# Order of TensorE's work in the attention loop: the former item's products with the values ahead of the turning of the present item's probabilities

## The chip, the cores and the metric
The kernel runs on one core of one Trainium2 chip. Its time is that of one execution on the device in microseconds (us); a lower time is better. Three runs of the kernel before took 3362.86, 3367.79 and 3368.50 us, the median is 3367.79.

## What is computed
The reference runs two blocks over 256 tokens of width 1024, two layers each: modulated norms, mixers, dense feed-forwards and a mixture of experts. What matters here is attention, which stands in it in five forms: neighbourhood attention of 256 latent tokens over 256 latent and 256 context tokens, dense attention of the 256 context tokens, window attention with a sink, difference attention, and dilated attention in three groups. Each is of this form, per head and query:

```python
s = jnp.einsum('bhqd,bhkd->bhqk', q, k) * d ** -0.5 + bias
m = s.max(-1, keepdims=True)
e = jnp.exp(s - m)
p = e / e.sum(-1, keepdims=True)
o = jnp.einsum('bhqk,bhkd->bhqd', p.astype(v.dtype), v)
```

## The kernel before, in words
The program is written out by hand for each engine, and the engines meet at semaphores. SyncE loads weights in units of up to 1 MB into four buffers (`raw`), ScalarE rounds them to a high part, VectorE forms the low part, and TensorE multiplies activations with both. This weight stream fills most of the time (L302, L307, L356 to L360). It stands still in the attention loops, with its buffers full.

Attention is done in items. An item is one head, 128 queries (so two items per head) and all keys that these see. `attn_pe`, `attn_dve` and `attn_act` (from L948, L995 and L1023) are the same loop seen from TensorE, VectorE and ScalarE. They run five times, on lists made by `even_items` (E0: 16 items of 512 keys with a bias; E1: 16 of 256), `window_items` (W: 16 of 512 with a mask), `diff_items` (D: 16 of 512) and `dilated_items` (A: 24 of 128, then 24 of 256, two extra matmuls each). An item i passes through these steps:

- S(i), TensorE, `scores` (L963, L965): queries by keys into one of two PSUM banks `SC`, then the bias or mask is added by more matmuls.
- maximum, VectorE (L1015; in W L1012 and L1013, with the sink's floor).
- exponential, ScalarE (L1030), from PSUM into one of two tiles `prob`, with its sum read out after it.
- T(i), TensorE (L989): `prob` is turned in pieces of 128 x 128 into one of two PSUM banks `PT`.
- copy, VectorE (`take`, L1006): `PT` into one of two tiles `probT` in SBUF.
- O(i), TensorE, `outputs` (L976): `probT` is the operand that is loaded as weights, the values stream past it, and the result is added up in PSUM.

The tiles `prob` and `probT` lie in `tmp`, so the trace calls them tmp. A float32 matmul stands as two records in the trace, so O of four pieces stands as x8, and O of two pieces as x4.

The order on TensorE is that of the loop in `attn_pe`: S(0), then for each i S(i+1), T(i), O(i-1), and O of the last item at the end. VectorE's order is maximum of i, copy of i-1, maximum of i+1. In between it has other work at some items, given by `every`: in E0, E1 and D, after items 4 and 6, it splits a finished pair of operands for the next projection (L932, L933), and in A it carries a finished group of eight heads out of PSUM after items 9, 17, 25, 33 and 41 (L2000). After a loop VectorE normalises the results (from L1222, L1435 or L2011 on), having waited for the last O, and TensorE turns them (`heads_out_pe`, L1235) for the next projection.

TensorE's waits in the loop: S(i) waits until the exponential of i-2 has read its bank; T(i) for the exponential of i and, from i = 2, for the copy of i-2, which has read its bank; O(i) for the copy of i.

Of the kernel before, what the change touches and what calls it, by code (L numbers as in the profile page):

```python
# [134 lines left out]
def program(nc, a, out, plan):  # L135
# [6 lines left out]
    def sem(name):  # L142
        if name not in sems:
            sems[name] = ctx.enter_context(nc.semaphore(name))
        return sems[name]
# [802 lines left out]
    def attn_pe(e, base, items, ready, *deps):  # L948

        e.after(*deps)  # L950
        last = len(items)

        def scores(i):
            it = items[i]
            if ready:
                ready(e, i)
            if i >= 2:

                e.eng.wait_ge(sem("exp_done"), base + i - 1)
            bank = SC[i % 2]  # L960
            n = it["n"]
            adds = it["adds"]
            nc_last = nc.tensor.matmul(bank[:, 0:n], it["q"], it["k"], start=True, stop=not adds)  # L963
            for j, (l_, r_) in enumerate(adds):
                nc_last = nc.tensor.matmul(bank[:, 0:r_.shape[-1]], l_, r_, start=False, stop=j == len(adds) - 1)  # L965
            nc_last.then_inc(sem("scores"), 1)

        def outputs(i):
            it = items[i]

            e.eng.wait_ge(sem("probT_done"), base + i + 1)
            if it.get("o_free"):
                it["o_free"](e)
            kt = it["n"] // P
            for k in range(kt):
                ins = nc.tensor.matmul(it["o"], probT[i % 2][:, k * P:k * P + P], it["v"][k],  # L976
                                       start=k == 0, stop=k == kt - 1)
            ins.then_inc(sem("out_ready"), 1)

        scores(0)  # L980
        for i in range(last):
            if i + 1 < last:
                scores(i + 1)

            e.eng.wait_ge(sem("exp_done"), base + i + 1)
            if i >= 2:
                e.eng.wait_ge(sem("probT_done"), base + i - 1)
            for k in range(items[i]["n"] // P):
                ins = nc.tensor.transpose(PT[i % 2][:, k * P:k * P + P], prob[i % 2][:, k * P:k * P + P], ident)  # L989
            ins.then_inc(sem("prob_turned"), 1)  # L990
            if i >= 1:
                outputs(i - 1)
        outputs(last - 1)

    def attn_dve(e, base, items, floor, *deps, every=None):  # L995
# [1050 lines left out]
    with ctx:  # L2046
# [272 lines left out]
        def _(pe):  # L2319
# [13 lines left out]
            for st in range(2):  # L2333
                if st:
                    conv_pe(e, 1)

                def ready(e, i):
                    if st == 0 and i % NT == 0:
                        e.after(f"bias{i // NT}")
                attn_pe(e, ATT0[st], E_ITEMS[st], ready, "qkT1", f"convT{st}", "even zeros", f"odd zeros{st}")  # L2340
                heads_out_pe(e, f"att_e{st}")
                follow(e, s, f"cat_e{st}")
                project_pe(e, s, [(xhi, xlo, KD)], D, f"out_e{st}")
                resid_pe(e, f"res_e{st}", (pick_lat, pick_ctx)[st], 0)
# [6 lines left out]
            if on(3):  # L2351
                mod_pe(e, s, 1, f)
                for st, n in enumerate((OW, OW - OQ)):
                    norm_pe(e, f"in_o{st}")
                    follow(e, s, f"in_o{st}")
                    project_pe(e, s, [(xhi, xlo, KD)], n, f"in_o{st}", late_pe(e, s, 1, st))
                odd_qk_pe(e)
                attn_pe(e, ATT0[2], W_ITEMS, None, "ckT", "dkT")
                heads_out_pe(e, "att_w")
                attn_pe(e, ATT0[3], D_ITEMS, None, "att_w:oT")  # L2360
                heads_out_pe(e, "att_d")
                follow(e, s, "cat_o")
                project_pe(e, s, [(xhi, xlo, KD)], D, "out_o")
                resid_pe(e, "res_o", pick_lat, 0)
# [69 lines left out]
```

## Time and profile before

| | |
|---|---|
| median of three runs | 3367.79 us |
| profiled execution: its time, its span | 3368.8 us, 3366.9 us |
| busy: TensorE, VectorE, ScalarE | 89%, 57%, 47% of the span |
| TensorE's mean granted clock | 0.935 of full speed |
| loops, from the first S to the last O started, read in the order of time | E0 273 to 319, E1 367 to 394, W 1074 to 1129, D 1134 to 1180, A 3063 to 3124 us |

Rows of the order in time give the start of a group of records in us, its length, its engine (PE is TensorE's matmuls, PEld its weight loads, DVE VectorE, ACT ScalarE), line, operation, what is written from what, sizes, and how many records it joins; in brackets stands how long the engine had been idle before it, and what ended that. The length goes from the first start to the last end, and matmuls overlap: the next group starts before the former one ends.

### The profile page before, as it was taken

To read this page: it belongs to the slowest core of one execution; us is meant where nothing else is said; L and a number is where in the kernel's file an instruction comes from. 1 tells how busy PE (TensorE), PEld (TensorE's weight loads), DVE (VectorE), ACT (ScalarE), POOL (GpSimd) and SP (SyncE) were. 2 spreads that over 40 slices of the span, in tenths; PEclk is the share of its full clock that TensorE was granted. 3 is DMA by queue.
4 is the path that set the end of the run, shared out by engine and by line. 5 is a ranking of instruction groups with operands and counts; after the bars stand their busy time and mean duration, and the time that the engine had idled before them with its cause. 6 is when DMAs were issued, how large, how long until landed. Compare 5 with 4: busy or idle time off the path is not lost.

```text
span 3366.9 us, 37398 instructions
## 1 busy us (share of the span) xinstructions
PE 3007.6 (89%) x14027; PEld 2483.2 (74%) x14027; DVE 1912.1 (57%) x2235; ACT 1578.0 (47%) x2125; POOL 148.9 (4%) x195
## 2 busy tenths in 40 slices
PE   6997799899686979999999989989778989898698
PEld 5775578787474658888888878867667878787587
DVE  5565555556456456666666665546555555544555
ACT  4553344444453235555555544455434444445344
POOL 1002000000111000000000000000000000000000
PEclk8998899999787979999999999989889999999899
DMA  7571245456752025555556555534024544551243
GB/s 262 199 238 50 67 156 173 160 167 205 188 187 100 1 66 190 179 171 186 187 182 195 187 163 181 186 130 138 1 71 167 179 164 162 200 183 62 81 158 142
DMA packets 266638, 510.49 MB, mean 152 GB/s; under 512 B 9497, under 2 KB 40449, under 8 KB 266528
## 3 DMA queue, kind: packets, MB, share of 16 engines
q1 hardware_dynamic: 262576, 498.11, 44.5%
q0 software_dynamic: 3952, 10.89, 1.6%
q8 instruction: 72, 1.18, 0.1%
q14 instruction: 38, 0.31, 0.0%
HBM read 507.91 MB, written 1.05 MB: 151 GB/s over the span
## 4 chain that ended last, share of the span: by engine, by line
PE 83%; DVE 8%; ACT 4%; DMA 2%; POOL 1%; issue 1%; DVEq 0%; ACTq 0%; POOLq 0%
PE bank L356 24%; PE bank L357 23%; PE bank L360 23%; PE bank L963 2%; PE bank L976 2%; DVE wlo L307 2%; PE bank L1599 2%; PE bank L433 1%; PE bank L989 1%; DMA raw<-in_od_w_in 1%; ACT whi L302 1%; PE bank L738 1%; PE bank L965 1%; POOL ss L679 1%; PE bank L866 1%
## 5 line engine op out<-in xcount | busy, mean ns | idle before, releaser
L307 DVE TENSOR_TENSOR wlo<-raw,whi 128x1024 fp32r<-128x1024 f32 x1044 | 1267.9, 1224 | 984.1 <-ACT whi L302 978.9
L302 ACT ACTIVATE whi<-raw 128x1024 fp32r<-128x1024 f32 x1044 | 1098.6, 1060 | 1030.4 <-PE bank L360 975.6
L356 PE MATMUL bank<-whi,xhi 128*128 128x512 f32 (+2 forms) x2672 | 1024.1, 383 | 53.9 <-DVE wlo L307 34.4
L357 PE MATMUL bank<-wlo,xhi 128*128 128x512 f32 (+2 forms) x2672 | 1015.2, 380 | 0.0
L360 PE MATMUL bank<-whi,xlo 128*128 128x512 f32 (+2 forms) x2672 | 1014.0, 379 | 0.0
L356 PEld LDWEIGHTS bank<-whi,xhi 128*128 128x128 f32 x2672 | 511.7, 192 | 150.8 <-issue 52.7
L360 PEld LDWEIGHTS bank<-whi,xlo 128*128 128x128 f32 x2672 | 511.3, 191 | 89.0
L357 PEld LDWEIGHTS bank<-wlo,xhi 128*128 128x128 f32 x2672 | 512.2, 192 | 86.4
L356 PE MATMUL bank<-whi,f_hhi 128*128 128x512 f32 x880 | 350.0, 398 | 0.0
L360 PE MATMUL bank<-whi,f_hlo 128*128 128x512 f32 x880 | 348.8, 396 | 0.0
L357 PE MATMUL bank<-wlo,f_hhi 128*128 128x512 f32 x880 | 348.8, 396 | 0.0
L360 PEld LDWEIGHTS bank<-whi,f_hlo 128*128 128x128 f32 x880 | 165.7, 188 | 40.4
L357 PEld LDWEIGHTS bank<-wlo,f_hhi 128*128 128x128 f32 x880 | 165.8, 188 | 39.2
L356 PEld LDWEIGHTS bank<-whi,f_hhi 128*128 128x128 f32 x880 | 165.8, 188 | 39.1
L738 PE MATMUL bank<-kb,tmp 128*128 128x128 f32 x224 | 51.1, 421 | 100.1 <-DVE tmp L718 100.1
L517 DVE TENSOR_TENSOR f_hlo<-bank,f_hhi 128x512 fp32r<-128x512 f32 (+1 forms) x114 | 71.6, 668 | 120.1 <-ACT f_hhi L479 120.1
L1030 ACT ACTIVATE tmp<-bank,negm 128x512 f32<-128x512 f32 (+2 forms) x112 | 60.7, 542 | 149.2 <-DVE negm L1015 110.2
L738 PEld LDWEIGHTS bank<-kb,tmp 128*128 128x128 f32 x224 | 45.1, 224 | 107.9 <-DVE tmp L718 107.6
L479 ACT ACTIVATE f_hhi<-bank 128x512 fp32r<-128x512 f32 (+1 forms) x114 | 60.6, 581 | 127.4 <-PE bank L433 127.4
L356 PE MATMUL bank<-whi,spad 128*128 128x512 f32 x192 | 83.0, 432 | 24.7 <-DVE wlo L307 24.1
L489 ACT ACTIVATE tmp<-bank 128x512 f32<-128x512 f32 (+2 forms) x120 | 60.9, 561 | 66.9 <-PE bank L360 66.8
L1015 DVE TENSOR_REDUCE negm<-bank 128x1 f32<-128x256 f32 (+2 forms) x96 | 46.0, 480 | 74.1 <-PE bank L965 45.3
(377 smaller groups left out, 2229.9 us busy)
## 6 DMA issues: line engine op xcount, KB each, us to landing
raw<-in_ffn_w SPq DMA_DIRECT2D x180, 1024.0 KB, 5.0
raw<-in_moe_w SPq DMA_DIRECT2D x64, 1024.0 KB, 5.1
raw<-in_moe_w SPq DMA_DIRECT2D x80, 768.0 KB, 4.4
raw<-in_ada_w SPq DMA_DIRECT2D x48, 1024.0 KB, 5.2
raw<-in_ev_w_in SPq DMA_DIRECT2D x24, 1024.0 KB, 5.8
raw<-in_ffn_w SPq DMA_DIRECT2D x36, 512.0 KB, 3.6
raw<-in_hyb_w_in SPq DMA_DIRECT2D x18, 1024.0 KB, 4.8
raw<-in_attn_w_qkv SPq DMA_DIRECT2D x18, 1024.0 KB, 4.9
```

Source lines behind the costliest of these rows:

```text
L302: nc.scalar.activation(whi[s][:, :, :], raw[slot][:, 2 * j:2 * j + 2, :], ACT.Copy)\
L307: nc.vector.tensor_tensor(wlo[s][:, :, :], raw[slot][:, 2 * j:2 * j + 2, :], whi[s][:, :, :].bitcast(F32), ALU.subtract)\
L356: nc.tensor.matmul(bank[:, 0:n], xk_h, whi[s][:, wk, 0:n], start=first, stop=False)
L357: ins = nc.tensor.matmul(bank[:, 0:n], xk_h, wlo[s][:, wk, 0:n], start=False, stop=last and xl is None)
L360: ins = nc.tensor.matmul(bank[:, 0:n], xk_l, whi[s][:, wk, 0:n], start=False, stop=last)
L489: ins = nc.scalar.activation(sg[:, t, 0:n], G[t][:, 0:n], ACT.Silu)
L517: ins = nc.vector.tensor_tensor(hlo[:, at, :].rearrange(flat), T[b // TOK][:, 0:k * TOK], hhi[:, at, :].bitcast(F32).rearrange(flat), ALU. ...
L738: ins = nc.tensor.transpose(banks[b][:, c:c + P], tmp[:, t, kk * P:kk * P + P], ident)
L963: nc_last = nc.tensor.matmul(bank[:, 0:n], it["q"], it["k"], start=True, stop=not adds)
L976: ins = nc.tensor.matmul(it["o"], probT[i % 2][:, k * P:k * P + P], it["v"][k], start=k == 0, stop=k == kt - 1)
L1030: nc.scalar.activation(prob[i % 2][:, 0:it["n"]], SC[i % 2][:, 0:it["n"]], ACT.Exp, bias=negm[:, i:i + 1], accum_out=den[:, i:i + 1]).then ...
L1599: ins = nc.tensor.matmul(to, diagonal_tap(k, j), hpad[:, k, j:j + TOK], start=j == 0, stop=j == TAPS - 1)
```

## The change
In TensorE's loop O(i-1) moves ahead of T(i), so that the order is S(i+1), O(i-1), T(i). T's own wait for the copy of i-2 goes; O(i-2), which now always stands before T(i), has made that wait. The other engines' programs are as before.

```diff
@@ -981,15 +981,13 @@
         for i in range(last):
             if i + 1 < last:
                 scores(i + 1)
+            if i >= 1:
+                outputs(i - 1)
 
             e.eng.wait_ge(sem("exp_done"), base + i + 1)
-            if i >= 2:
-                e.eng.wait_ge(sem("probT_done"), base + i - 1)
             for k in range(items[i]["n"] // P):
                 ins = nc.tensor.transpose(PT[i % 2][:, k * P:k * P + P], prob[i % 2][:, k * P:k * P + P], ident)
             ins.then_inc(sem("prob_turned"), 1)
-            if i >= 1:
-                outputs(i - 1)
         outputs(last - 1)
```

## Rows read from the trace of the kernel before

**Rows 1.** The page's chain that ended last: shares of the span by engine.

```profile
PE 83%; DVE 8%; ACT 4%; DMA 2%; POOL 1%; issue 1%; DVEq 0%; ACTq 0%; POOLq 0%
```

**Rows 2.** Waits in E1, then A: engine, tile, line waited for: us, times, longest.

```profile
PEld bank L989 <- ACT tmp L1030: 8.1, 11, 3.5
...
PEld bank L989 <- ACT tmp L1030: 6.9, 16, 1.6
```

**Rows 3.** Order in time, E1, within the loop.

```profile
377.13 0.38 PE L989 MATMUL bank<-kb,tmp 128*128 128x128 f32 x2
...
377.67 0.41 DVE L1006 COPY tmp<-bank 128x256 f32<-128x256 f32 x1
...
379.40 0.41 DVE L1006 COPY tmp<-bank 128x256 f32<-128x256 f32 x1
...
388.23 0.61 PE L976 MATMUL bank<-e_p,tmp 128*128 128x128 f32 x4
...
388.67 0.60 PE L963 MATMUL bank<-e_kT,e_qT 128*128 128x256 f32 x2
...
389.11 0.38 PE L989 MATMUL bank<-kb,tmp 128*128 128x128 f32 x2
...
389.32 0.61 PE L976 MATMUL bank<-e_p,tmp 128*128 128x128 f32 x4
...
391.54 0.38 PE L989 MATMUL bank<-kb,tmp 128*128 128x128 f32 x2
```

**Rows 4.** Order in time, the end of E1.

```profile
392.82 0.44 PE L989 MATMUL bank<-kb,tmp 128*128 128x128 f32 x2 [0.45 <-ACT tmp L1030]
...
393.29 0.42 DVE L1006 COPY tmp<-bank 128x256 f32<-128x256 f32 x1 [0.80 <-PE bank L989]
...
393.77 0.52 PEld L976 LDWEIGHTS bank<-e_p,tmp 128*128 128x128 f32 x4 [0.26 <-DVE tmp L1006]
```

**Rows 5.** Order in time, A, items of 128 keys.

```profile
3070.44 0.33 PE L989 MATMUL bank<-kb,tmp 128*128 128x128 f32 x1
...
3077.84 0.29 DVE L1006 COPY tmp<-bank 128x128 f32<-128x128 f32 x1 [0.52 <-PE bank L989]
...
3090.00 0.27 PE L989 MATMUL bank<-kb,tmp 128*128 128x128 f32 x1
```

**Rows 6.** Order in time, A, items of 256 keys.

```profile
3092.45 0.38 PE L989 MATMUL bank<-kb,tmp 128*128 128x128 f32 x2
...
3102.69 0.41 DVE L1006 COPY tmp<-bank 128x256 f32<-128x256 f32 x1
...
3104.28 0.41 DVE L1006 COPY tmp<-bank 128x256 f32<-128x256 f32 x1
...
3121.36 0.38 PE L989 MATMUL bank<-kb,tmp 128*128 128x128 f32 x2
```

**Rows 7.** Order in time, the end of D.

```profile
1173.52 0.66 PE L989 MATMUL bank<-kb,tmp 128*128 128x128 f32 x4
...
1176.06 0.66 PE L989 MATMUL bank<-kb,tmp 128*128 128x128 f32 x4
...
1177.72 0.66 PE L989 MATMUL bank<-kb,tmp 128*128 128x128 f32 x4
...
1179.16 0.71 PE L976 MATMUL bank<-o_pl,tmp 128*128 128x128 f32 x4
```

**Rows 8.** Order in time, the ends of E0 and W.

```profile
314.93 0.60 PE L989 MATMUL bank<-kb,tmp 128*128 128x128 f32 x4
...
317.18 2.10 PE L976 MATMUL bank<-e_p,tmp 128*128 128x128 f32 x16
...
1124.57 0.60 PE L989 MATMUL bank<-kb,tmp 128*128 128x128 f32 x4
...
1127.96 0.71 PE L976 MATMUL bank<-o_pl,tmp 128*128 128x128 f32 x4
```

**Rows 9.** Busy us of PE, PEld, DVE, ACT, POOL in E1; PEclk, DMA share, GB/s.

```profile
382.00:384.00 2.00, 1.47 (x11) 1.07 (x10) 1.52 (x5) 1.13 (x4) 0.00 (x0) 1.00 0.02 4
```

## The prediction

> **What bounds the kernel now.** First the chain of waits of the whole execution: TensorE holds 83% of it [rows 1], so time is lost or won where TensorE waits. The change touches only the attention loop, which runs five times: 16 items of 512 keys with biases (call it E0), 16 of 256 (E1), 16 of 512 with a mask (W), 16 of 512 (D), and 24 of 128 followed by 24 of 256 (A). S(i), T(i) and O(i) are the scores, the turning and the products with the values of item i. Between them lie VectorE's maximum, ScalarE's exponential (before T), and VectorE's copy out of PSUM (between T and O).
>
> Next the waits by releaser in two of these loops: T's weight load waits for the exponential 8.1 us in E1 (11 times, the first 3.5) and 6.9 us in A (16 times, one of 1.6) [rows 2]. So where items are short, the return S, maximum, exponential, T ends last now. The loops of 512 keys show hardly any such wait within the loop: they are paced by TensorE's own work.
>
> Last the order in time. At the full clock E1's TensorE work per item is O 0.44 us (388.23 to 388.67), S 0.44 (to 389.11), T 0.21 (to 389.32), together 1.09 [rows 3]. The laps it takes are longer: from T at 377.13 to T at 391.54 are 11 laps in 14.41 us, 1.31 each [rows 3]. In A, 20 laps of 128 keys take 19.56 us (3070.44 to 3090.00), 0.98 each [rows 5], and 21 laps of 256 take 28.91 us (3092.45 to 3121.36), 1.38 each [rows 6]. D laps in 2.54 us (1173.52 to 1176.06) [rows 7].
>
> **What moves.** Before, the queue is S(i+1), T(i), O(i-1); after, S(i+1), O(i-1), T(i). No instruction but one semaphore wait is dropped (T's wait for the copy, which O, now ahead of it, makes anyway); I cost that at nothing, since the matmuls of a lap already stand back to back [rows 3]. No DMA moves, nothing passes another queue of SP's or POOL's, and VectorE's and ScalarE's lists are untouched. In either order TensorE does the same work.
>
> Two returns change length. The exponential gets one O more to hide behind: good. The copy loses cover: O(i-1) had S(i+1) and T(i) ahead of it after T(i-1), now only S(i+1). And as T(i) stands behind the waiting O(i-1), what is queued behind that wait is T(i), S(i+2), then VectorE's copy of i and its next maximum. The new cycle is T, copy, O, T.
>
> **How long the copy's return is.** The loop's end in E1 shows it bare: T starts at 392.82, the copy at 393.29 (0.42 long), the next O's load at 393.77 [rows 4], so 0.95 us. That T carries 0.06 for its own late weight load (0.44 recorded against 0.38 in a T not kept waiting [rows 3, 4]). An O that waited takes 0.10 before its first matmul (0.71 recorded for four at 1179.16 [rows 7], 0.61 for four in rows 3). So from an unhindered T to its O: 0.95 - 0.06 + 0.10 = 0.99 us at 256 keys. At 512: 1179.16 - 1177.72 = 1.44 [rows 7], less 0.06, plus 0.10: 1.48. At 128: one transpose fewer (0.21/2, say 0.11) and a copy of 0.29 instead of 0.42 [rows 4, 5]: 0.99 - 0.24 = 0.75.
>
> The lap can then not be under O plus this return: 0.44 + 0.99 = 1.43 us at 256, 0.22 + 0.75 = 0.97 at 128, 0.88 + 1.48 = 2.36 at 512. The last is under D's 2.54, so in D nothing changes, and E0 and W, which add a bias or mask matmul to the same lap, have more room. The short loops are now paced by the copy.
>
> - E1: 11 laps at 1.43 are 15.73 us. In two laps VectorE also splits a pair of operands between two copies: copy to copy takes 1.73 us there (377.67 to 379.40 [rows 3]), 0.30 over 1.43, twice. 15.73 + 0.60 - 14.41 = **+1.9 us**.
> - A, 128 keys: 20 x 0.97 = 19.4. Twice VectorE carries results out between two copies; at 256 keys copy to copy is then 1.59 us (3102.69 to 3104.28 [rows 6]), at 128 some 0.26 less (a copy and a maximum, 0.13 each), 1.33, so 0.36 over, twice. 19.4 + 0.7 - 19.56 = **+0.5 us**.
> - A, 256 keys: 21 x 1.43 = 30.03, plus three times 0.16 for that carrying, less 28.91: **+1.6 us**.
>
> Where a loop starts at half clock, I put nothing: T's and S's 0.65 doubled is 1.30, an estimate, about what the return takes there, since only its transposes double.
>
> **The loop's end.** The last T has no S behind which the copy before it can hide. Counted from the T that stands right after the last S, before: last O's first matmul at 393.77 + 0.10 in E1 with T at 391.54 [rows 3, 4]. After, four steps follow one another from there: O, return, O, return, that is 391.54 + 0.44 + 0.99 + 0.44 + 0.99 = 394.40 against 393.87: +0.5. A ends alike: +0.5. At 512 keys the four steps are 2 x (0.88 + 1.48) = 4.72. E0: 314.93 + 4.72 = 319.65, against the last eight matmuls, which end at 317.18 + 2.10 and last 1.06 like any eight (0.61 for four plus four more at 0.11): 318.22 [rows 8]: +1.4. W: 1124.57 + 4.72 = 1129.29 against 1127.96 + 0.10 [rows 8]: +1.2. D: 1176.06 + 4.72 = 1180.78 against 1179.26 [rows 7]: +1.5. Together **+5.1 us**. Nothing covers this, since VectorE's normalisation waits for the last O; the weights of the next projection lie ready, so no DMA absorbs it.
>
> **Sum.** 1.9 + 0.5 + 1.6 + 5.1 = +9.1 us on the profiled execution's 3368.8, which stands 1.0 above the median of 3367.79: 3377 us. Bounds: without the 0.10 for O's load the 52 laps and ten returns give back 6.2 us (+2.9); with handovers 0.05 longer in each they add 3.1 (+12.2). E0 may lose up to 0.5 more where its splits fall between copies. A change under about 0.2%, 6.7 us, cannot be told from none here.
>
> The Trainium skill ("TensorE: Matmul & The Clock Gate", Part 2, step by step) says that TensorE pulls weight loads ahead of matmuls in flight. By that rule O's load would be ready when its turn comes and the sum would be the lower bound, +2.9. The trace does not agree at a wait: the O at 1179.16 records 0.10 more than others [rows 7].
>
> **Rivals.**
> (a) *Loads hidden*: O's load does not show, perhaps because the wait is passed while S still streams. For it: at 256 keys in A a load that starts 0.1 before S ends costs nothing. Against: the rows just named. +2.9: 3371, no measurable change.
> (b) *The exponential's wait was all*: the copy returns behind S, and all waits of rows 2 but the first ones go: 8.1 - 3.5 + 6.9 - 1.6 = 9.9 us, less the ends' 5.1: -4.8, 3363, not slower. It decides if T to O takes less than T plus S, 0.21 + 0.44 = 0.65 in E1. Against: 0.95 measured bare.
> (c) *The clock falls*: short idles in each lap bring TensorE to half clock in E1, 2 x 1.09 = 2.18 instead of 1.43 us, 11 times: +8 more, 3385; in A more still. Against: from 382 to 384 us TensorE was busy 1.47 of 2 us and kept the full clock [rows 9], and a lap of 1.09 in 1.43 is about as dense. The Trainium skill (same page, "A second HAM failure mode: psum-queue depth-cycling") tells of such small idles between matmul groups letting the clock swing; by it the time would be (c)'s, and rows 9 do not agree.
> That the change does nothing is excluded for the ends; in E0, W and D it is what I expect within the loop.
>
> **Chances.** Forecast 0.70 (3372 to 3383), (a) 0.15, (b) 0.06, (c) 0.09. The range 3370 to 3387 takes in (a) and the cheap form of (c). Of the forecast's own range a tenth is below 3374.5. So faster by over 0.2%: 0.03 (half of (b)); within: 0.25; slower: 0.72.
>
> **What would show it.** Right: the waits of O's load for the copy (L976 for L1006) become the largest of TensorE in E1 and A, those of L989 for L1030 vanish but for the first; copy to copy 1.43 and 0.97; D's lap still 2.54; from the last S to the last O longer by 1.2 to 1.5 us in E0, W and D. Wrong: laps of 1.1 in E1 (then (b)), 1.33 there and in A (then (a)), a clock below 1 there (c), or D's lap changed.

## The result, and the profile after

| kernel | median, us (runs) | against before: difference of medians; ratio, 95% interval |
|---|---|---|
| before, first series | 3368.31 (18) | |
| after, first series | 3374.64 (18) | +6.3; 1.0017 [1.0011, 1.0024] |
| before, second series | 3368.76 (27) | |
| after, second series | 3380.06 (11) | +11.3; 1.0029 [1.0020, 1.0038] |
| after, profiled execution: its time, its span | 3371.37, 3369.4 | before 3368.8, 3366.9 |

The change makes the kernel slower by 0.17% in one series of runs and 0.29% in the other. The forecast of +9.1 us, a ratio of 1.0027, lies just above the first interval and inside the second. The ratio is not exactly that of the two medians (in the second series they give 1.0034); by the ratio the second difference is +9.8 us. Stretches of the program that the change does not touch also differ between executions: from the end of E1 to the start of W the profiled executions show 679.41 us before, 676.87 after, 684.03 in the second profile of after. So the loops themselves are the finer measure. Each is read in the order of time, from the first record of S to the first VectorE instruction that the last O released:

| us | E0 | E1 | W | D | A | sum |
|---|---|---|---|---|---|---|
| before | 46.21 | 27.62 | 55.28 | 45.66 | 60.81 | 235.58 |
| after | 47.64 | 30.23 | 55.26 | 47.52 | 64.19 | 244.84 (+9.3) |
| after, second profile | 47.63 | 30.55 | 56.47 | 47.65 | 64.22 | 246.52 (+10.9) |
| forecast of the difference | +1.4 | +2.4 | +1.2 | +1.5 | +2.6 | +9.1 |

The chain that ended last shows nothing of it; rounded to whole per cents it is that of [rows 1]:

```profile
PE 83%; DVE 8%; ACT 4%; DMA 2%; POOL 1%; issue 1%; DVEq 0%; ACTq 0%; POOLq 0%
```

The waits of after's weight loads in E1 (first two lines) and A (last two), with the columns of [rows 2]; in the changed kernel's listing the copy is L1004 and the exponential L1028:

```profile
PEld bank L976 <- DVE tmp L1004: 8.6, 16, 0.8
PEld bank L989 <- ACT tmp L1028: 3.5, 1, 3.5
...
PEld bank L976 <- DVE tmp L1004: 3.0, 7, 0.8
PEld bank L989 <- ACT tmp L1028: 1.6, 1, 1.6
```

Set beside [rows 2], this is the exchange the prediction described. T's wait for the exponential is gone in both loops but for the first item's (3.5 and 1.6 us), and in E1 each of the 16 O's now waits for its copy, 8.6 us against the 4.6 that went (8.1 - 3.5). In A the sum of O's waits is small, 3.0 us in 7 of 48; the laps say more there than this list.

The order in time of after, in E1:

```profile
387.21 0.38 PE L989 MATMUL bank<-kb,tmp 128*128 128x128 f32 x2
...
387.63 0.42 DVE L1004 COPY tmp<-bank 128x256 f32<-128x256 f32 x1 [0.59 <-PE bank L989]
...
388.11 0.52 PEld L976 LDWEIGHTS bank<-e_p,tmp 128*128 128x128 f32 x4 [0.48 <-DVE tmp L1004]
388.11 0.71 PE L976 MATMUL bank<-e_p,tmp 128*128 128x128 f32 x4
...
388.66 0.38 PE L989 MATMUL bank<-kb,tmp 128*128 128x128 f32 x2
```

This is the cycle T, copy, O, T: T at 387.21, the copy from 387.63 to 388.05, O's load at 388.11, T again at 388.66. One lap is 1.45 us, of which 0.90 from T to O's load, 0.10 for that load and 0.44 for O (with rounding). S went in between and did not fill the time. The load's group and the matmul's start at the same 388.11, so this load had no matmul to hide behind. In the same stretch TensorE was busy 1.64 of 2 us, and the granted clock was 1.00 (the columns of [rows 9]):

```profile
384.00:386.00 2.00, 1.64 (x13) 1.24 (x13) 1.50 (x4) 1.04 (x4) 0.00 (x0) 1.00 0.00 0
```

The order in time of after, in A: first an item of 128 keys, then one of 256.

```profile
3081.45 0.27 PE L989 MATMUL bank<-kb,tmp 128*128 128x128 f32 x1
...
3081.76 0.29 DVE L1004 COPY tmp<-bank 128x128 f32<-128x128 f32 x1 [0.29 <-PE bank L989]
...
3082.10 0.49 PE L976 MATMUL bank<-a_p,tmp 128*128 128x128 f32 x2
...
3082.43 0.27 PE L989 MATMUL bank<-kb,tmp 128*128 128x128 f32 x1
...
3101.55 0.38 PE L989 MATMUL bank<-kb,tmp 128*128 128x128 f32 x2
...
3101.97 0.42 DVE L1004 COPY tmp<-bank 128x256 f32<-128x256 f32 x1 [0.35 <-PE bank L989]
...
3102.33 0.28 PE L965 MATMUL bank<-a_dil,a_one 128*128 128x256 f32 x1
3102.45 0.52 PEld L976 LDWEIGHTS bank<-a_p,tmp 128*128 128x128 f32 x4
3102.45 0.71 PE L976 MATMUL bank<-a_p,tmp 128*128 128x128 f32 x4
...
3103.00 0.38 PE L989 MATMUL bank<-kb,tmp 128*128 128x128 f32 x2
```

The laps are 0.98 and 1.45 us (before they alternated between 0.78 and 1.04, and were 1.33). At 256 keys S with its two extra matmuls nearly fills the copy's return: its last matmul starts at 3102.33, O's load at 3102.45, 0.06 after the copy's end (3102.39), and no idle time is recorded before it. That is why the list of waits shows so little for A. The lap is longer than before by 0.12 all the same: the load that stands bare, 0.10, and a hundredth or two of waiting. (In e4 below, where the copy had long been done, O's load behind the same S starts 0.11 before its matmul, and the lap is 1.33.) From 3094.19 to 3124.97 the 21 laps take 30.78 us, and 20 laps of 128 keys 20.34 (3071.29 to 3091.63).

The ends of E1 and of E0 in after, in the order of time:

```profile
395.90 0.38 PE L989 MATMUL bank<-kb,tmp 128*128 128x128 f32 x2
...
396.79 0.52 PEld L976 LDWEIGHTS bank<-e_p,tmp 128*128 128x128 f32 x4 [0.75 <-DVE tmp L1004]
...
397.34 0.38 PE L989 MATMUL bank<-kb,tmp 128*128 128x128 f32 x2
...
398.24 0.52 PEld L976 LDWEIGHTS bank<-e_p,tmp 128*128 128x128 f32 x4 [0.75 <-DVE tmp L1004]
...
398.99 0.25 DVE L1220 RECIPROCAL den<-den 128x16 f32<-128x16 f32 x1 [0.80 <-PE bank L976]
```

```profile
316.59 0.60 PE L989 MATMUL bank<-kb,tmp 128*128 128x128 f32 x4
317.23 0.69 DVE L1004 COPY tmp<-bank 128x512 f32<-128x512 f32 x1 [0.64 <-PE bank L989]
317.97 1.16 PE L976 MATMUL bank<-e_p,tmp 128*128 128x128 f32 x8 [0.78 <-DVE tmp L1004]
318.97 0.60 PE L989 MATMUL bank<-kb,tmp 128*128 128x128 f32 x4
...
320.35 1.16 PE L976 MATMUL bank<-e_p,tmp 128*128 128x128 f32 x8 [0.78 <-DVE tmp L1004]
321.55 0.25 DVE L1220 RECIPROCAL den<-den 128x16 f32<-128x16 f32 x1 [1.25 <-PE bank L976]
```

Each shows return, O, return, O in a row, where before the last two O's of E0 stood as one group of sixteen records [rows 8]. In E0 TensorE stands idle 0.78 us twice, and the normalisation (L1220) starts only after the second O.

### The profile page after: what moved, and what is told of

It is laid out like the page before. It is cut to its first block, busy times and chain, and to the rows that moved or that the text cites. A ratio compares the mean times of both kernels' runs of the same rounds, so it can differ in the third digit from the quotient of the medians.

```text
span 3369.4 us, 37296 instructions
## 1 busy us (share of the span) xinstructions
PE 3010.4 (89%) x14027; PEld 2485.8 (74%) x14027; DVE 1916.9 (57%) x2235; ACT 1577.8 (47%) x2125; POOL 148.4 (4%) x195
## 4 chain that ended last, share of the span: by engine, by line
PE 83%; DVE 8%; ACT 4%; DMA 2%; POOL 1%; issue 1%; DVEq 0%; ACTq 0%; POOLq 0%
PE bank L356 24%; PE bank L357 23%; PE bank L360 23%; PE bank L976 2%; PE bank L963 2%; DVE wlo L307 2%; PE bank L1597 2%; PE bank L433 1%; ACT whi L302 1%; DMA raw<-in_od_w_in 1%; PE bank L989 1%; PE bank L738 1%; PE bank L965 1%; POOL ss L679 1%; PE bank L866 1%
## 5 line engine op out<-in xcount | busy, mean ns | idle before, releaser
L1028 ACT ACTIVATE tmp<-bank,negm 128x512 f32<-128x512 f32 (+2 forms) x112 | 60.7, 542 | 152.8 <-DVE negm L1013 115.3
L1004 DVE COPY tmp<-bank 128x512 f32<-128x512 f32 (+2 forms) x112 | 57.0, 509 | 59.1 <-PE bank L989 58.8
```

The costliest lines, as they stand in the source:

```text
L1028: nc.scalar.activation(prob[i % 2][:, 0:it["n"]], SC[i % 2][:, 0:it["n"]], ACT.Exp, bias=negm[:, i:i + 1], accum_out=den[:, i:i + 1]).then ...
```

## The experiments

Two theories went into the runs. Mine: the copy's return now paces the short loops, and it stands bare at the end of every loop. The rival: the loss is a matter of where TensorE's work lies in the long loops, of the clock, or of something outside the loops. Three kernels split the change, two stretch the copy, three give both returns cover, one repeats the change. In e1, e2 and e3 `early(i)` chooses, per item, whether O(i-1) stands ahead of T(i) or behind it, and T keeps its wait for the copy of i-2.

### e1_long: the new order in E0, W and D alone

```diff
+        early = lambda i: base in (0, 32, 48)
...
-            if i >= 1:
+            if i >= 1 and early(i):
                 outputs(i - 1)
```

> The new order only in the three loops of 512 keys (E0, W, D); E1 and A keep the old one. Theory (the copy's return TensorE, VectorE, TensorE paces short laps, and each loop's end loses its cover): the laps of E0 and W stay at 2.62 and 3.01 us, D's at 2.58 (the trace after), E1 and A have the old laps; only the ends cost, 1.4 + 1.2 + 1.5 us, and D's laps 0.5: about +4.6 us on the kernel before. Rival (what the change costs comes from the short loops alone, the ends are absorbed by what follows): 0.

Measured: 3372.38 us against 3368.27, ratio 1.0007 [0.9998, 1.0016], which alone cannot be told from no change. The loops: E0 47.63, W 55.26, D 47.62, the sum with E1 and A +3.6. E0's +1.42 and D's +1.96 are those of after; E1 (27.84) and A (60.83) stand within 0.3 of before. W's did not show, for a reason given below.

### e2_short: the new order in E1 and A alone

```diff
+        early = lambda i: base in (16, 64)
```

> The new order only in E1 and A, the loops of 256 and 128 keys. Theory: laps of 1.45 us in E1, 0.98 and 1.45 in A, as in the trace after, and two ends at 0.5: +1.9 + 0.5 + 1.6 + 1.0, about +5.0 us on the kernel before. Rival (the ends of the long loops are all that counts): +1.

Measured: 3373.42 us, ratio 1.0018 [1.0009, 1.0027]; the loops +6.5. E1 30.27 and A 64.32, as in after, with E0 at 46.21 and D at 45.67 as before. So the short loops lose with no help from the long ones, and the parts add up: 3.6 + 6.5 = 10.1 us, between after's +9.3 and +10.9. (Of the 6.5, 0.4 is W's, which keeps the old order here.)

### e3_end: the new order, but the last item in the old one

```diff
+        early = lambda i: i < last - 1
```

> The new order in all loops, except that the last item of each keeps the old one: T of the last item stands ahead of O of the one before it, so that this O covers the last copy, and the last S's successor is T again. Theory: the ends give back 5.1 us and the laps stay as after, so about +4 us on the kernel before, and 5 less than the kernel after. Rival (the ends do not count): as after, +6.

Measured: 3371.05 us, ratio 1.0007 [0.9998, 1.0016]; the loops +5.5, 3.8 less than after. From the last S to the release by the last O it shows 5.68, 3.42, 6.24, 5.52 and 3.66 us in E0, E1, W, D and A; before had 5.68, 3.41, 6.23, 5.36 and 3.65. All five ends but D's are back to a hundredth. By whole loops after lost 1.47, 0.68, 1.10 and 0.53 us more than this kernel in E0, E1, D and A, 3.8 together, and W gave nothing (55.28 against 55.26). That is close to the 3.9 put for these four ends, but by chance: whole loops also hold how each execution began them, and e3 reached the fourth T of E1 0.22 us and the third T of D 0.39 us later than after did (W's start is told below). From the last S to the release alone, after takes 1.46, 0.90, 1.26, 1.49 and 0.66 us more than e3, 5.8 together, against a forecast of 5.1; in E1 and A this stretch also holds a part of a lap's wait. The ratio alone cannot be told from no change here either.

### e5_after_copy2 and e6_before_copy2: the copy done twice, in the new and in the old order

```diff
+            e.link(nc.vector.tensor_copy(probT[i % 2][:, 0:n], PT[i % 2][:, 0:n]))
             e.link(nc.vector.tensor_copy(probT[i % 2][:, 0:n], PT[i % 2][:, 0:n]))
```

> The kernel after, with VectorE's copy from PSUM done twice, the second after the first (its result is the same). Theory (in the new order the lap is O plus T-to-O, and holds the copy in full): the lap grows by the copy wherever that cycle is the longer: E1 from 1.45 to about 1.9 us, A from 0.98 to 1.3 and from 1.45 to 1.9; at 512 keys the cycle goes from 2.36 to about 3.1, so D from 2.58 to 3.1, E0 from 2.62 to 3.1, W from 3.01 to hardly more than 3.1. Rival (TensorE sets the laps): D, E0 and W unchanged.

> The kernel before, with the same doubled copy. Theory: the copy has S and T as cover, so in E0, W and D the laps stay at 2.62, 3.01 and 2.54 us; in E1 and A, where the copy stands ahead of the next maximum on VectorE, the laps may grow by up to a copy of 0.3 to 0.4. Rival (the copy counts in full in either order): E0, W and D grow by 0.5 as in the kernel after.

Measured, one execution each: 3425.41 us for the new order, 3374.32 for the old one, 3367.85 for before. The same extra work on VectorE costs 54 us in the new order (3425.41 - 3371.37, both profiled executions), and 6 in the old one. The five loops hold 46 and 5 us of it; the other 8 us of the new order lie outside them and are not explained. The laps of the new order became 1.91 in E1, 1.31 and 1.90 in A, and 3.10 in each of E0, W and D, three loops that had laps of 2.62, 3.01 and 2.58. In the old order E0, W and D stayed at 2.62, 3.01 and 2.54; its 5 us are mainly E1's (+1.1) and A's (+3.0), mostly from laps in which VectorE also has other work, and from longer ends. The order in time of e5_after_copy2 in D:

```profile
1193.12 0.60 PE L989 MATMUL bank<-kb,tmp 128*128 128x128 f32 x4
...
1193.76 0.69 DVE L1004 COPY tmp<-bank 128x512 f32<-128x512 f32 x1 [1.09 <-PE bank L989]
1194.48 0.69 DVE L1005 COPY tmp<-bank 128x512 f32<-128x512 f32 x1
...
1195.23 0.71 PE L976 MATMUL bank<-o_pl,tmp 128*128 128x128 f32 x4 [0.46 <-DVE tmp L1005]
```

From copy to copy 0.72 us. The prediction's bound for 512 keys, O 0.88 plus return 1.48, plus this 0.72 is 3.08; the lap is 3.10, whatever S and its biases take. At 256 keys the second copy adds 0.46 and at 128 keys 0.33, so the bounds are 1.89 and 1.30, and the laps 1.91 and 1.31. This is the cycle named in the prediction, made the bound in all five loops by one edit.

### e4_lag2: O two items behind, in every loop

```diff
-            if i >= 1:
-                outputs(i - 1)
+            if i >= 2:
+                outputs(i - 2)
...
+        outputs(last - 2)
         outputs(last - 1)
```

> O goes back one item further: S(i+1), O(i-2), T(i). Then neither return stands bare: the exponential has T, S and an O to hide behind, as after, and the copy has S, O, T and S. The buffers are the same two. Theory (two returns, whichever is short of cover paces the lap): E1 laps at TensorE's own 1.09 us, A at 0.77 and 1.33, no wait of T or O within the loops, E0, W and D unchanged; the ends as in the kernel before or shorter. 11 x 0.22 + 20 x 0.21 + 21 x 0.05, about 7.5 us less than the kernel before, some 14 less than after. Rival (the laps are paced by TensorE's own starting up after each wait, or by VectorE, and not by the two returns): within 2 us of the kernel before.

Measured: 3365.25 us, ratio 0.9991 [0.9982, 1.0000]. This gives the exponential S and O to hide behind, as the change wanted, and the copy a whole lap. E1's steady lap fell to 1.10, its TensorE work of 1.09, and the waits of O's load for the copy went from E1's list. T's load waits for the exponential in 4 cases, one of them the first (3.5 us), the rest mostly where splits hold VectorE up:

```profile
PEld bank L988 <- ACT tmp L1028: 5.1, 4, 3.5
```

But the gain was 3.0 us by the medians, 0.4 of the expected 7.5, and the loops of the profiled execution do not even show that: they sum to 237.0 us, 1.4 more than before, while the rest of that execution was 7.4 us shorter than before's. So the 3.0 us cannot be put down to the loops. A took 61.39 us instead of 60.81: its steady laps were at TensorE's work (0.78 to 0.83, and 1.33), while three of 256 keys took 2.20 and two of 128 keys 1.96. The order in time of e4_lag2 in such a lap:

```profile
3085.22 0.88 DVE L1998 COPY y<-bank 128x256 f32<-128x256 f32 x2 [0.46 <-PE bank L976]
...
3086.13 0.42 DVE L1013 TENSOR_REDUCE negm<-bank 128x1 f32<-128x256 f32 x1
...
3086.59 0.47 ACT L1028 ACTIVATE tmp<-bank,negm 128x256 f32<-128x256 f32 x1 [1.80 <-DVE negm L1013]
...
3087.21 0.44 PE L988 MATMUL bank<-kb,tmp 128*128 128x128 f32 x2 [0.70 <-ACT tmp L1028]
```

VectorE carries out a finished group after items 9, 17 and so on, once the last O of that group is there. With O one item later VectorE first waited for it (idle 0.46 before the 0.88 us of copies), its next maximum came late, and the exponential (idle 1.80) and T behind it. I had moved an O and not looked at who waits for it. W and D lost too (+0.85 and +1.75): D's laps are 2.58 as in after, and in both loops more of the first laps ran at half clock.

### e7_mixed and e8_lag2_carry: the same with the carrying one item later

e8 is e4 with this edit; e7 has O two items behind in E0, E1 and A only (`base in (0, 16, 64)`) and the order of before, with its wait, in W and D.

```diff
-            if i >= 9 and (i - 9) % 8 == 0:
-                raw_take((i - 9) // 8)
+            if i >= 10 and (i - 10) % 8 == 0:
+                raw_take((i - 10) // 8)
```

> S(i+1), O(i-2), T(i) in E0, E1 and A, the old order in W and D, and in A VectorE carries a finished group out one item later (10, 18, 26, 34, 42 instead of 9, 17, ...), so that it does not wait for the O that now comes an item later. Theory: E0's end gives 0.5 us and E1 1.3 as in the run with O two items back everywhere; in A the five laps with a carrying fall from 1.96 and 2.20 to about 1.35 and 1.55 us, so A ends 2.6 us under the kernel before; W and D as before. Together 4.4 us under the kernel before. Rival (the five long laps come from something other than that wait): 1 us under it.

> O two items back in all five loops, with the carrying one item later. Theory: as the mixed kernel, but D's laps at 2.58 instead of 2.54 us (13 laps, 0.5 us) and more of the first items of W and D at half clock, 3 us less gain in one execution's trace: 2 to 4 us under the kernel before. Rival: the earlier gain of this order came from somewhere else than the loops, then 3 us under as measured there.

Measured: e7 3363.10 us, ratio 0.9984 [0.9975, 0.9993]; e8 3362.65, ratio 0.9978 [0.9969, 0.9987]. Both are faster than before and than after. A fell from e4's 61.39 to 57.91 and 58.02 us: the laps with a carrying are 1.48 and 1.41 instead of 1.96 and 2.20. In e7 the loops sum to 230.44, 5.1 less than before (E0 -0.5, E1 -1.7, A -2.9, W and D unchanged), close to the medians' 5.7. In e8 W and D take 2.8 us more than in e7, the sum -1.7, yet its median is no higher; it lies 6.1 us under before, outside the expected 2 to 4, and the loops do not account for the rest. The two intervals overlap, and the runs do not tell which of them is the better.

### e9_after_again: the changed kernel once more

> The kernel after once more, to see how much of its loops' 9.3 us (read from its trace against that of the kernel before) the whole time shows. If the loops' cost comes out in full, its ratio lies near 1.0027 (+9), and the loops of this execution cost 9 to 10 us again; if some 3 us are given back outside the loops, near 1.0017 (+6), with stretches outside the loops shorter than in the kernel before again.

Measured: 3380.06 us, ratio 1.0029 [1.0020, 1.0038], the loops +10.9. E0, E1, D and A repeat those of the first profile of after within 0.32 us; the largest difference, 1.21, is in W.

## Why the prediction was right, point by point

**Direction and mechanism were right.** The copy's return set the laps of the short loops, and e5 shows it: it lengthens this return alone, and the laps of all five loops follow by the formula, to 0.02 us.

**The laps.** Forecast 1.43, 0.97 and 1.43 us; measured 1.45, 0.98 and 1.45. E1's 11 laps from 379.43 to 395.90 take 16.47 us, +2.06 where the forecast had +1.9. A gained 0.78 and 1.87 where it had 0.5 and 1.6. The cycle was short by 0.01 to 0.02 per lap, and over some 50 laps that is most of the 0.7 us missing.

**O's load at a wait, 0.10 us.** Confirmed: 0.71 us recorded for the four at 388.11 and 3102.45, against 0.61 without a wait. The steady lap of 1.33 of rival (a) did not appear in E1 or, at 256 keys, in A. The Trainium skill ("TensorE: Matmul & The Clock Gate", Part 2, step by step) has loads pulled ahead of matmuls in flight. The traces agree where nothing is waited for: in e4's E1, T's first load starts 0.11 before its matmul (378.50 and 378.61), and O's 0.21 (382.00 and 382.21). They don't where a load waits for the copy: at 388.11 load and matmul start together.

**The ends.** Forecast +5.1 us. E0 gained 1.43 with laps unchanged, and W's end grew by 1.26 (forecast 1.4 and 1.2). In E1 the loop's +2.61 less the laps' 2.06 leaves 0.55, for 0.5. Counted from the place right behind the last S, as the prediction counts, D's end grew by 1.54 and A's by 0.55, for 1.5 and 0.5. Together +5.3. e3, which restores the ends alone, takes 5.8 us less from the last S on, with a part of a lap's wait in it.

**D's lap: the one term of the sum that failed.** I wrote that D's 2.54 exceeds the 2.36 of the cycle, "so in D nothing changes", and named a changed lap of D as a sign of being wrong. The lap is 2.58. The order in time of after in D:

```profile
1176.59 0.60 PE L989 MATMUL bank<-kb,tmp 128*128 128x128 f32 x4
...
1177.12 1.12 PE L963 MATMUL bank<-o_kT,o_qT 64*128 64x512 f32 x2
1177.22 0.69 DVE L1004 COPY tmp<-bank 128x512 f32<-128x512 f32 x1 [0.83 <-PE bank L989]
...
1178.17 0.52 PEld L976 LDWEIGHTS bank<-o_pl,tmp 128*128 128x128 f32 x4 [0.76 <-DVE tmp L1004]
1178.17 0.71 PE L976 MATMUL bank<-o_pl,tmp 128*128 128x128 f32 x4
```

The copy ended at 1177.91, 0.26 us before the load that is put down to it, so it was not waited for. What stands before this load is S, here with operands of 64 rows. Right behind it the first load shows in either order: T recorded 0.66 instead of 0.60 before [rows 7], O records 0.71 instead of 0.61 now. The difference of the two, 0.04, is the lap's 0.04. Over 12 laps (1148.23 to 1179.16, 30.93 us, before 30.41 from 1145.65 to 1176.06) that is +0.5 us, a term that the sum lacks. e4, where the copy has a whole lap of cover, shows 2.58 as well, so it is no wait. That the rows of the operand are what matters is a reading. It is borne out by the loads that follow S in the other loops of after, E0 (S of 128 rows, 512 keys) and W (S of 64 rows, 512 keys):

```profile
296.06 1.02 PE L963 MATMUL bank<-e_kT,e_qT 128*128 128x512 f32 x2
296.50 0.19 PEld L965 LDWEIGHTS bank<-e_bias,kb 128*128 128x128 f32 x1 [0.24 <-issue]
...
1102.56 1.12 PE L963 MATMUL bank<-o_kT,o_qT 64*128 64x512 f32 x2
1103.61 0.30 PEld L965 LDWEIGHTS bank<-o_band,kb 128*128 128x128 f32 x2 [0.76 <-issue]
1103.62 0.70 PE L965 MATMUL bank<-o_band,kb 128*128 128x256 f32 x2
```

Behind 128 rows the bias's load starts 0.43 us before its matmul at 296.93; behind 64 rows the mask's load starts with its matmul. In W that bare load stands in either order, and its lap of 3.01 did not change. No kernel changed the rows alone.

**W's part.** Its end came as forecast (7.49 us after the last S began, before 6.23), but the loop's total stayed. The start of W in before, in the order of time:

```profile
1073.93 2.07 PE L963 MATMUL bank<-o_kT,o_qT 64*128 64x512 f32 x2 [2.80 <-ACT o_kT L1412]
```

and in after:

```profile
1075.86 1.12 PE L963 MATMUL bank<-o_kT,o_qT 64*128 64x512 f32 x2 [3.22 <-ACT o_kT L1410]
```

The same S took 2.07 us in one and 1.12 in the other; the granted clock of the 2 us from its start was 0.50 and 0.97. From it to the first T are 6.16 us in before, 4.53 in after and 4.33 in e1, but 6.17 in after's second profile and in e3. Among those that began like before, after's second profile has 56.47 for the loop, before 55.28, and e3, with the old order at the end alone, 55.28 again: +1.19 and -1.19, the forecast's 1.2. After and e1, which began at the full clock, have 55.26 both. The same code of after shows either start, so the change is not needed for it. The loop in the old order varies as well, from 54.76 (e6, though its end holds the doubled copy) to 55.64 us (e2), so W's term in a single pair of profiles is uncertain by half its size or more.

**The removed semaphore wait, at nothing.** Nothing speaks against it: e2 drops no wait and has E1 and A as in after to 0.13 us.

**The other rivals.** (b), that the exponential's wait was all, would have given laps of 1.1 in E1. They came in e4, where the copy has cover, and not in after: its condition was the right one, and T to O, 0.90 before the load, was far above 0.65. (c), the half clock, did not come: the granted clock was 1.00 from 378 us to the end of E1 and from 3072 us to the end of A. The Trainium skill (same page, "A second HAM failure mode: psum-queue depth-cycling") tells of another kernel whose clock swung with small idles between its groups of matmuls; this kernel's steady laps do not show that.

**What the views were to show.** Right for both lists of waits in E1 and for the exponential's in A. Not for O's in A, which I had expected to be clearly TensorE's largest (3.0 us, no more than the first S's single wait), and D's stretch from the last S on grew by 1.65, above the stated 1.2 to 1.5: a load may set the lap, bare and on time to 0.01 us, and leave no idle time to be listed.

**The size at the stopwatch.** +6.3 and +9.8 us (the second by its ratio) stand around the +9.1. The loops gave +9.3 and +10.9. The rest of the program took 6.8 us less in the first profile of after than in before (spans +2.4, loops +9.3) and 0.2 more in the second; this isn't explained by these runs. That the first profile's +9.3 lies so close to +9.1 is partly luck: the terms as measured are +4.7 for the laps of E1 and A, +0.5 for D's and +5.3 for the ends, +10.6 in all, and the first profile shows less because W and D began 1.3 and 0.2 us faster than in before (A 0.2 slower). The forecast was some 1.5 us short.

## What to carry to other kernels

In a software pipeline across engines, write down every return (here scores to exponential to turning, and turning to copy to products) with what stands beside it on the waiting engine. Moving an instruction takes cover from one return to give it to the other; a lag of one item more gave cover to both, and two kernels with it were faster than before (0.9978 and 0.9984), once the carrying that waits for the moved O was moved along. The loops account for the gain of e7, 5.1 of 5.7 us, and not for all of e8's. Count the loop's end separately: there nothing follows that could hide a return, and here that was half of the loss, spread over five loops.

## What was not expected of the hardware

- Behind S with operands of 64 rows, in D, O's load shows with no wait: 0.10 us, against 0.06 for T's, 0.04 per lap (2.58 against 2.54).
- The list of waits names the copy for D's loads (11.9 us in 15), though in 13 of the 15 it was done some 0.25 us earlier; only the two at the loop's end waited for it. A releaser that ended long before the wait did was not the one:

```profile
PEld bank L976 <- DVE tmp L1004: 11.9, 15, 1.0
```

- One and the same code started W at a granted clock of 0.50 or 0.97, 1.6 us apart by the first T; a loop of 55 us read in a single profile moved by 1.2 us with it.
